# Top-2 choice by rank, with softmax weights and record addresses made on GpSimd, in a one-layer hybrid decoder kernel

## The reference, cut to what matters

```python
x = layer_norm(alpha * x + concat(attention, hgrn2) @ w_o, ln1_g, ln1_b)
g_prob = softmax(xt @ w_group + b_group)          # 4 groups
g_w, g_idx = top_k(g_prob, 1)
e_logits = expert logits of the chosen group      # 4 of 16 experts
e_w, e_idx = top_k(softmax(e_logits), 2)          # two experts
w_tok = g_w * e_w / sum(e_w)
for e in range(16):
    y += combine[:, e] * ((silu(xt @ w_gate[e]) * (xt @ w_up[e])) @ w_down[e])
x = layer_norm(alpha * x + y, ln2_g, ln2_b)
```

## Time and profile before

| | |
|---|---|
| median of 3 runs | 619.57 us (618.94 to 619.57) |
| the profiled execution | 618.28 us |
| its span, first to last instruction | 616.5 us |
| TensorE busy | 594.3 us (96%) |
| VectorE busy | 478.2 us (78%) |
| ScalarE busy | 373.8 us (61%) |
| GpSimd busy | 128.4 us (21%) |
| mean granted TensorE clock | 0.989 |

### The profile page before, as it was taken

How to read it: one execution, slowest core, us unless ns; L and a number is a source line. 1 busy time by engine, 2 the same in 40 slices (tenths; PEclk the granted TensorE clock), 3 DMA queues, 4 the chain that set the end, 5 groups by cost and what they waited for, 6 DMA issues and landing times.

```text
span 616.5 us, 9761 instructions
## 1 busy us (share of the span) xinstructions
PE 594.3 (96%) x3691; PEld 478.2 (78%) x3691; DVE 478.2 (78%) x572; ACT 373.8 (61%) x401; POOL 128.4 (21%) x111
## 2 busy tenths in 40 slices
PE   9999999999999999999799999999999999999990
PEld 7878888888887678877588888888888888888870
DVE  3758598794577765546898889888888988888867
ACT  3659434432215984213378887877887787787735
POOL 0004222290000440000483532111111011111000
PEclk9999999999999999999899999999999999999996
DMA  9831133223206003975699999999999999999664
GB/s 327 295 99 60 62 131 118 84 72 77 71 2 204 2 3 114 419 281 209 231 394 419 418 366 372 392 388 389 408 408 391 388 389 388 392 411 403 222 171 136
DMA packets 42557, 155.77 MB, mean 253 GB/s; under 512 B 11939, under 2 KB 12147, under 8 KB 30236
## 3 DMA queue, kind: packets, MB, share of 16 engines
q1 hardware_dynamic: 37500, 138.40, 57.4%
q0 software_dynamic: 5024, 16.92, 10.6%
HBM read 139.96 MB, written 15.34 MB: 252 GB/s over the span
## 4 chain that ended last, share of the span: by engine, by line
PE 87%; DMA 5%; DVE 4%; issue 2%; ACT 2%; DVEq 0%; POOLq 0%
PE psum L659 25%; PE psum L661 23%; PE psum L660 23%; DMA acc_dram<-misc,slots 3%; PE psum L772 2%; PE psum L1054 2%; PE psum L912 2%; PE psum L889 2%; DMA ring<-acc_dram 1%; PE psum L1071 1%; PE psum L876 1%; PE psum L668 1%; ACT ring L1313 1%; PE psum L814 1%; DMA misc<-x_dram,first 1%
## 5 line engine op out<-in xcount | busy, mean ns | idle before, releaser
L1776 DVE TENSOR_TENSOR w_lo<-ring,w_hi 128x2048 fp32r<-128x2048 f32 x95 | 216.5, 2294 | 23.7 <-ACT w_hi L1346 23.6
L659 PE MATMUL psum<-w_hi,act_hi 128*128 128x512 f32 x544 | 219.1, 403 | 1.5 <-DVE act_lo L1935 1.0
L661 PE MATMUL psum<-w_hi,act_lo 128*128 128x512 f32 x544 | 212.6, 391 | 0.0
L660 PE MATMUL psum<-w_lo,act_hi 128*128 128x512 f32 x544 | 212.3, 390 | 0.0
L1346 ACT ACTIVATE w_hi<-ring 128x2048 fp32r<-128x2048 f32 x96 | 182.1, 1916 | 25.1 <-PE psum L661 25.1
L659 PEld LDWEIGHTS psum<-w_hi,act_hi 128*128 128x128 f32 x544 | 102.3, 188 | 28.2 <-DVE w_lo L1776 4.7
L661 PEld LDWEIGHTS psum<-w_hi,act_lo 128*128 128x128 f32 x544 | 102.1, 188 | 22.1
L660 PEld LDWEIGHTS psum<-w_lo,act_hi 128*128 128x128 f32 x544 | 102.3, 188 | 19.2
L613 POOL DMA_INDIRECT acc_dram<-misc,slots x15 | 25.6, 1706 | 193.6 <-ACT misc L1396 176.0
L1194 ACT ACTIVATE w_hi<-ring 128x2048 fp32r<-128x2048 f32 x17 | 32.6, 1918 | 49.1 <-PE psum L661 47.4
L1505 DVE TENSOR_TENSOR w_lo<-ring,w_hi 128x2048 fp32r<-128x2048 f32 x17 | 39.8, 2344 | 22.3 <-ACT w_hi L1194 22.1
(11 more groups left out here) (246 smaller groups left out, 687.1 us busy)
## 6 DMA issues: line engine op xcount, KB each, us to landing
ring<-in_w_gate SPq DMA_DIRECT2D x32, 1024.0 KB, 17.4
ring<-in_w_up SPq DMA_DIRECT2D x32, 1024.0 KB, 18.3
ring<-in_w_down SPq DMA_DIRECT2D x32, 1024.0 KB, 18.7
ring<-in_w_in SPq DMA_DIRECT2D x13, 1024.0 KB
ring<-in_w_o SPq DMA_DIRECT2D x4, 1024.0 KB
acc_dram<-ring SPq DMA_DIRECT2D x5, 512.0 KB, 4.0
ring<-in_x SPq DMA_DIRECT2D x2, 1024.0 KB, 6.5
ring<-strip_dram SPq DMA_DIRECT2D x8, 256.0 KB, 4.4
```

The source lines that it names most:

```text
L659: pe.matmul(dst, lh, rh, start=first, stop=False, skip_group_check=True)
L660: pe.matmul(dst, lh, rl, start=False, stop=False, skip_group_check=True)
L661: return pe.matmul(dst, ll, rh, start=False, stop=last, skip_group_check=True)
L1776: dve.tensor_tensor(w_lo[:, v0 % WBUF, :], ring[:, slot, :], w_hi[:, v0 % WBUF, :].bitcast(F32), ALU.subtract).then_inc(s_lo, 1)
```

## The change

The choice is made by counting: for each value, how many of its group of four beat it (ties go to the earlier). Rank below 0.5 is the first choice, 1 the second, below 1.5 both. VectorE does this in three instructions per pair of tiles; the pair 0 and 1 goes ahead of the last half residual. GpSimd makes the exponents' input, the addresses and the weights' sum in a chain of 26 instructions behind gather 1, each of which waits for the one before it; ScalarE's Exp waits for the twelfth, VectorE's reciprocal (now ahead of unit 3) for the twenty-fifth. VectorE splits units 0 and 1 where it made weights and addresses. The diff, but for the offsets of the constants:

```diff
@@ -84,8 +84,8 @@
     for l, m in enumerate(LEVELS):
         c[:, C_MASK + 64 * (l + 1):C_MASK + 64 * (l + 2)] = (s // (2 * m) == t // (2 * m)) & (s % (2 * m) < m) & (t % (2 * m) >= m)
     c[:, C_SCAN:C_SCAN + SEQ] = (np.arange(SEQ) % CH != 0)[None]
-    c[:, C_W4:C_W4 + 4] = [4, 3, 2, 1]
-    c[:, C_E16:C_E16 + NE] = np.arange(NE)
+    c[:, C_TIE:C_TIE + 16] = [0 if i < j else np.finfo(np.float32).tiny for j in range(4) for i in range(4)]
+    c[:, C_E16:C_E16 + NE] = np.arange(NE) - NE
     for i in range(T):
         tok = i * P + np.arange(P)
         for k in range(2):
...
@@ -294,9 +294,13 @@
             return v.rearrange("p (%s) -> p %s" % (" ".join(names), " ".join(names)), **dict(zip(names, shape)))
 
         r_msk = msk_b[:, :].rearrange("p (i e) -> p i e", i=T)
-        r_l, r_hot, r_top, r_first = rcol(T, NL), rcol(T, NL), rcol(T * (1 + NG), 1), rcol(T * (1 + NG), 1)
-        r_l2, r_hot2, r_top2, r_first2 = rcol(T, NE), rcol(T, NE), rcol(T * NG, 1), rcol(T * NG, 1)
-        r_x, r_d, r_both, r_gsum, r_gw, r_q = rcol(T, NG + 1), rcol(T, NG), rcol(T, NE), rcol(T, 1), rcol(T, 1), rcol(T, 1)
+        r_l, r_group, r_hot, r_hot2, r_top = rcol(T, NL), rcol(T, NG), rcol(T, NE), rcol(T, NE), rcol(T, 1)
+        r_rank, r_beats, r_step = rcol(T, NL), rcol(2 * (1 + NG), 4, 4), rcol(T, NE)
+        r_x, r_gsum, r_q = rcol(T, NG + 1), rcol(T, 1), rcol(T, 1)
+        def four(v):
+            return v.rearrange("p t (g e) -> p t g e", g=NG)
+
+        group_four = r_group.rearrange("p t (g a) -> p t g a", a=1).broadcast_to((P, T, NG, EPG))
         r_sel, r_pos, r_t16, r_at1, r_adr, r_cnt = rcol(2, T, NE), rcol(T, NE), rcol(2 * T, NE), rcol(T, NE), rcol(2 * T, 1), rcol(1)
 
 
...
@@ -593,8 +597,49 @@
             pool.wait_ge(s_slots, 2)
             gather(1)
 
+            pooled = [2]
+
+            def then(ins):
+
+                pooled[0] += 1
+                ins.then_inc(s_pool, 1)
+                pool.wait_ge(s_pool, pooled[0])
+
+            def folded(v, n, op):
+
+                while n > 1:
+                    n //= 2
+                    then(pool.tensor_tensor(v(0, n), v(0, n), v(n, 2 * n), op))
+
+            pool.wait_ge(s_rneed, 1)
+            pooled[0] = 4
+            pool.wait_ge(s_pool, 4)
+            then(pool.tensor_tensor(r_x[:, :, 0:NG], r_l[:, :, 0:NG], r_top.broadcast_to((P, T, NG)), ALU.subtract))
+            then(pool.tensor_scalar(r_hot, r_rank[:, :, NG:NL], 0.5, None, ALU.is_lt))
+            then(pool.tensor_scalar(r_hot2, r_rank[:, :, NG:NL], 1.0, None, ALU.is_equal))
+            then(pool.tensor_tensor(four(r_sel[:, 0]), four(r_hot), group_four, ALU.mult))
+            then(pool.tensor_tensor(four(r_sel[:, 1]), four(r_hot2), group_four, ALU.mult))
+            then(pool.tensor_tensor(r_step, r_sel[:, 1], r_sel[:, 0], ALU.subtract))
+            then(pool.tensor_tensor(r_step, r_step, r_l[:, :, NG:NL], ALU.mult))
+            folded(lambda a, b: r_step[:, :, a:b], NE, ALU.add)
+            pool.tensor_copy(r_x[:, :, NG:NG + 1], r_step[:, :, 0:1]).then_inc(s_rneed, 1)
+
+            e16 = cst[:, C_E16:C_E16 + NE].rearrange("p (a e) -> p a e", a=1)
+            then(pool.tensor_scalar(r_pos, r_at1, float(NE), None, ALU.mult))
+            then(pool.tensor_tensor(r_pos, r_pos, e16.broadcast_to((P, T, NE)), ALU.add))
+            for k in range(2):
+                then(pool.tensor_tensor(r_sel[:, k], r_sel[:, k], r_pos, ALU.mult))
+            sel = r_sel.rearrange("p k i e -> p (k i) e")
+            folded(lambda a, b: sel[:, :, a:b], NE, ALU.add)
+            then(pool.tensor_copy(addr_i[:, :, :].rearrange("p k i -> p (k i)").rearrange("p (n a) -> p n a", a=1), sel[:, :, 0:1]))
+            pool.wait_ge(s_rexp, 1)
+            folded(lambda a, b: r_x[:, :, a:b], NG, ALU.add)
+            then(pool.tensor_scalar(r_q, r_x[:, :, NG:NG + 1], ALPHA, ALPHA, ALU.mult, ALU.add))
+            pool.tensor_tensor(r_gsum, r_x[:, :, 0:1], r_q, ALU.mult).then_inc(s_addr, 1)
+
             pool.wait_ge(s_pads, 16 * (SEQ // P))
             pool.wait_ge(s_addr, 2)
+            then(pool.tensor_tensor(weight_of(rec_i[:, :, 1, 2:3]), weight_of(rec_i[:, :, 0, 2:3]), r_x[:, :, NG:NG + 1], ALU.mult))
             for n in range(2 * T):
                 if n == 5:
                     pool.wait_ge(s_slots, 3)
...
@@ -1372,7 +1417,7 @@
             logit_copy(T - 1)
             for v0 in range(3):
                 ehi(v0, 0)
-            act.wait_ge(s_rneed, 1)
+            act.wait_ge(s_rneed, 2)
             act.activation(r_x, r_x, ACT.Exp).then_inc(s_rexp, 1)
 
             def xt_hi(e, b):
...
@@ -1817,6 +1862,18 @@
                     residual(T - 1, 0)
                 if i >= 1:
                     link(logits_of(i - 1))
+
+            def ranks(t0):
+
+                ls = r_l[:, t0:t0 + 2, :].rearrange("p t (g e) -> p (t g) e", e=4)
+                shape = (P, 2 * (1 + NG), 4, 4)
+                link(dve.tensor_tensor(r_beats, ls.rearrange("p s (a i) -> p s a i", a=1).broadcast_to(shape),
+                                       ls.rearrange("p s (j a) -> p s j a", a=1).broadcast_to(shape), ALU.subtract))
+                tie = cst[:, C_TIE:C_TIE + 16].rearrange("p (a j i) -> p a j i", a=1, j=4)
+                link(dve.tensor_tensor(r_beats, r_beats, tie.broadcast_to(shape), ALU.is_ge))
+                link(dve.tensor_reduce(r_rank[:, t0:t0 + 2, :].rearrange("p t (g e a) -> p (t g) e a", e=4, a=1), r_beats, AX.X, ALU.add))
+
+            ranks(0)
             residual(T - 1, 1)
             moments(T - 1)
             last_in, last_out = x_res[:, T - 1, :], x1_out[:, T - 1, :]
...
@@ -1829,40 +1886,20 @@
 
 
             tokens = cst[:, C_REC:C_REC + 6 * T].rearrange("p (i a b) -> p i a b", i=T, a=1)[:, :, :, 0:1]
-            def bc(ap, n):
-                return ap.broadcast_to((P, T, n))
-
             link(logits_of(T - 1))
-            w4 = cst[:, C_W4:C_W4 + 4].rearrange("p (a n) -> p a n", a=1)
-
-            def first_max(values, hot, top, first, n):
-
-                values, hot = values.rearrange("p t (g e) -> p (t g) e", e=4), hot.rearrange("p t (g e) -> p (t g) e", e=4)
-                link(dve.tensor_reduce(top, values, AX.X, ALU.max))
-                link(dve.tensor_tensor(hot, values, top.broadcast_to((P, n, 4)), ALU.is_equal))
-                link(dve.tensor_tensor(hot, hot, w4.broadcast_to((P, n, 4)), ALU.mult))
-                link(dve.tensor_reduce(first, hot, AX.X, ALU.max))
-                link(dve.tensor_tensor(hot, hot, first.broadcast_to((P, n, 4)), ALU.is_equal))
-
-            first_max(r_l, r_hot, r_top, r_first, T * (1 + NG))
-            link(dve.scalar_tensor_tensor(out=r_l2, in0=r_hot[:, :, NG:NL], scalar=-BIG, in1=r_l[:, :, NG:NL], op0=ALU.mult, op1=ALU.add))
-            first_max(r_l2, r_hot2, r_top2, r_first2, T * NG)
-            group = r_hot[:, :, 0:NG]
-
-            def in_group(dst, src):
-                four = lambda v: v.rearrange("p t (g e) -> p t g e", g=NG)
-                return dve.tensor_tensor(four(dst), four(src), group.rearrange("p t (g a) -> p t g a", a=1).broadcast_to((P, T, NG, EPG)), ALU.mult)
-
-            link(dve.tensor_tensor(r_both, r_hot[:, :, NG:NL], r_hot2, ALU.add))
-            in_group(r_msk, r_both).then_inc(s_mask, 1)
+            ranks(T // 2)
+            link(dve.tensor_scalar(r_group, r_rank[:, :, 0:NG], 0.5, None, ALU.is_lt))
+
+            dve.scalar_tensor_tensor(out=four(r_msk), in0=four(r_rank[:, :, NG:NL]), scalar=1.5, in1=group_four,
+                                     op0=ALU.is_lt, op1=ALU.mult).then_inc(s_mask, 1)
             dve.wait_ge(s_used, MIX_UNITS)
             dve.tensor_copy(record[:, :, :, :], tokens.broadcast_to((P, T, NE, 2))).then_inc(s_rec, 1)
             dve.wait_ge(s_mask, 1)
+            dve.tensor_reduce(r_top, r_l[:, :, 0:NG], AX.X, ALU.max)
             dve.wait_ge(s_pos, 1)
             pos = psum[:, 7, 0:T * NE].rearrange("p (i e) -> p i e", i=T)
-            e16 = cst[:, C_E16:C_E16 + NE].rearrange("p (a e) -> p a e", a=1)
-
-            link(dve.scalar_tensor_tensor(out=r_at1, in0=pos, scalar=1.0, in1=r_msk, op0=ALU.add, op1=ALU.mult))
+            dve.scalar_tensor_tensor(out=r_at1, in0=pos, scalar=1.0, in1=r_msk, op0=ALU.add, op1=ALU.mult).then_inc(s_rneed, 1)
+            dve.wait_ge(s_rneed, 1)
 
             def place(e):
 
...
@@ -1879,25 +1916,8 @@
             place(1)
             slots_of(0, 1, 5)
             slots_of(1, 2, 3)
-            tops = r_top.rearrange("p (t g) a -> p t (g a)", t=T)
-            link(dve.tensor_tensor(r_x[:, :, 0:NG], r_l[:, :, 0:NG], tops[:, :, 0:1].broadcast_to((P, T, NG)), ALU.subtract))
-            link(dve.tensor_tensor(r_d, r_top2.rearrange("p (t g) a -> p t (g a)", t=T), tops[:, :, 1:1 + NG], ALU.subtract))
-            link(dve.tensor_tensor(r_d, r_d, group, ALU.mult))
-            dve.tensor_reduce(r_x[:, :, NG:NG + 1], r_d, AX.X, ALU.add).then_inc(s_rneed, 1)
-            in_group(r_sel[:, 0], r_hot[:, :, NG:NL])
```

(20 more changed lines are left out.)

## The result

| | before | after |
|---|---|---|
| median, runs side by side | 619.57 us | 622.84 us (622.50 to 625.04) |
| ratio | | 1.0063, 95% interval 1.0045 to 1.0082 |
| profiled execution, span | 616.5 us | 621.0 us |

Slower by 3.3 us, where +6.7 was forecast.

The account below looks back on a forecast made before the run. TensorE, busy 96% of 616.5 us, bounds it through its hole before the experts. Gather 2's wait (336.5 - 329.84 = +6.7) swallows the first shift and clock: 619.57 + 6.7 = 626.3 us, range 620.9 to 631.0.

Parts of the forecast that it names:

- the first wait: Before the experts: ScalarE's Exp waits for twelve GpSimd instructions, holding e_hi to 306.8 against 303.60; experts start 3.2 us later.
- the hold-up by the splits: GpSimd can't reach its data during VectorE's big subtractions; its first small instruction sits behind unit 1's until 301.6.
- rival 1: Only the Exp wait counts, gather 2 lands in time: +3.2, with the clock +5.1, 621 to 625 us; chance 0.25.
- second wait: At expert 2's transposes: gather 2, behind five scatters, issued near 327.5, lands 336.5 against 329.84, +6.7 us.
- Choice by rank: Router mask on VectorE: 3.39 us removed, 1.5 put in, 1.9 less; 1.57 passes the warming matmuls.
- Start of GpSimd's chain: Behind gather 1, ending near 300.2 in unit 0's split; the first small instruction sits behind unit 1's until 301.6.
- rival 3: Gather 0 is itself caught by unit 0's split, lands 2.3 us late, first shift +4.1; counted into forecast and rival 1.
- Size of the twelve instructions: GpSimd's twelve ahead of Exp: six at 0.53, six at 0.25 + 0.09, 5.2 us; bounds 3.2 and 7.1.
- first shift: Start of the expert matmuls: 3.2 us later than before, 3.2 to 5.1 with the low clock.
- Clock: TensorE's pause grows by 4.8 us; a low stretch on expert matmuls, 3.8 us at half rate, loses 1.9 us.
- After that: Slots' table, queued behind gather 2, moves 7 to 11 us, its need 6.7; within 5.8 us, no further wait.
- Faster rival: GpSimd not held by splits, twelve done by 303.3: 0.85 us faster, up to 1.57; 618.0 to 618.7 us; chance 0.10.

Follow-up runs that it names:

- unit 1 late: The changed kernel with the split of unit 1 moved back behind the first e_lo: 627.42 us, ratio 1.0134.
- warm gap: The changed kernel with 40 more warming matmuls between the first transposes and the wait for the first e_lo: 628.31 us, ratio 1.0158.
- Exp behind e_hi: The changed kernel with Exp and its wait moved behind both e_hi copies on ScalarE: 630.58 us, ratio 1.0185.
- gather 2 ahead: Gather 2 behind two scatters instead of five: 626.29 us in the changed kernel, 621.31 in that with the warm gap, 624.86 in that with Exp behind e_hi.
- choice by rank with more warming: The changed kernel without GpSimd's chain (VectorE makes its values, unit 1 split after first e_lo), plus 14 warming matmuls: 617.27 us, second set 616.91.

## Why the prediction was right, and where its sizes were off

The direction, the first wait and the hold-up by the splits were right. That the time lies in the range is owed to the range's lower part, which was there for rival 1: the forecast's own case, a second wait that takes TensorE to +6.7, did not occur in the change, and gather 2 came in time by 0.7 us only because the low clock had slowed everything around it. To that extent it was luck.

- **Choice by rank.** The mask was forecast at 293.9, it ended at 293.91. Of the 1.9 us, 1.57 were to pass the warming matmuls; gather 0 was issued at 296.69 (296.92 forecast), so it was 1.8.
- **Start of GpSimd's chain.** Forecast: gather 1 to 300.2, first instruction until 301.6. Measured: 300.01 and 301.44. The caught-gather case of rival 3 didn't happen; gather 0 took 1.06 us.
- **Size of the twelve instructions.** The term was too large. The eleven free ones were priced at 4.9 us and took 3.8: 0.30 to 0.32 for a two-input instruction of 64 elements instead of 0.44, with 0.08 between two. The 443 ns of the earlier trace rows belong to a form with a pointer to a scalar; the nearest here, with a constant, took 0.38. So e_hi came at 305.53, not 306.8, and the first shift was 1.9 us, not 3.2. A two-input GpSimd instruction at 0.30 stands against VectorE's 0.22, 1.4 times. The Trainium skill, GPSIMD Engine Reference, section Engine selection, has about twice. For all twelve, with no split beside them, the kernel with unit 1 late shows 4.2 us (300.33 to 304.49), where my sum had 5.2 and the estimate from the Trainium skill's ratio 5.8.
- **Clock.** A low stretch on expert matmuls was priced at 1.9 us, measured 2.3. With the first shift of 1.9 that is the 4.1 to 4.2 us by which the transposes of expert 2 were late; rival 1 had such a case at 5.1, with a first shift of 3.2.
- **The step that failed is the size of the second wait.** "Gather 2 is issued near 327.5" was 4.5 us too late: scatters started at 313.49 instead of 315.5, and up to the next issue the five took 9.5 us instead of 12.0. Two things made the start early: the cheaper chain, and that in the change ScalarE, held back with TensorE at the low clock, gave the hi of unit 3 late, so that GpSimd's last product (312.73, 0.21 us) passed before that split (rows below). With unit 1 late the same product stood behind the split for 2.12 us and the scatters began at 316.19; with the warm gap at 315.40. Later two of the five scatters went through in 0.96, as the splits were spread. Landing took 10.3 us, not 9. It landed 0.7 us ahead of need, so the wait itself was nil. The mechanism is real in nearby kernels: it decided three experiments (warm gap, Exp behind e_hi, unit 1 late) with 4.7 to 8.0 us, and there gather 2 was issued at 326.37, 329.91 and 326.80, around the forecast's 327.5. For the change itself rival 1 was the case that came true; I gave it 0.25. The timeline of VectorE of the changed kernel, then of GpSimd with unit 1 late:
```profile
314.31 2.29 DVE L1821 TENSOR_TENSOR w_lo<-ring,w_hi 128x2048 fp32r<-128x2048 f32 x1 [1.73 <-ACT w_hi L1391]
```
```profile
313.78 2.12 POOL L642 TENSOR_TENSOR rec_i<-rec_i,misc 128x4 f32<-128x4 f32 x1 [0.36 <-DVE rec_i L1962]
316.19 1.08 POOL L591 DMA_INDIRECT slot_dram<-rec_i,addr_i  x1 [0.29 <-POOL rec_i L642]
```
- **After that.** That the table of slots is no further wait was right for the change, with 3.4 us of room; the 2.46 us with gather 2 ahead show how near it is.
- **Faster rival.** It needed the twelve done by 303.3; they were done at 305.37. Even without the hold-up by the splits (unit 1 late) they ended at 304.49.

## What to carry to other kernels

Moving small work to an idle engine changes what stands in that engine's queue and in the queues of those that wait for it: here Exp was not urgent, but the copy behind it was, and a gather stood behind the scatters that needed the results. Before moving a step, list for each queue what is next behind the wait, and when it is needed. When several waits lie close in line, removing the first alone can cost time, because it also takes away the gaps in which the later ones caught up. Edits had to go together here: Exp or the clock with gather 2 to win back what each alone had lost (both stayed above before), choice by rank with more warming to beat before.

## What the runs showed of the hardware

- GpSimd's small instructions stand still while VectorE subtracts two on-chip tensors: 1.40 us against 0.23 for the same instruction. With two splits back to back (unit 1 late, 306.47 to 311.0) one instruction came through per split: two sums of pairs, started at 306.63 and 308.94, took 2.23 and 2.15 us.
- The hold-up can also fall on VectorE: beside a GpSimd product of 1024 elements (2.88 us, from 351.90 in the change) a split took 3.79 us instead of 2.29:
```profile
351.39 3.79 DVE L1821 TENSOR_TENSOR w_lo<-ring,w_hi 128x2048 fp32r<-128x2048 f32 x1 [0.43 <-ACT w_hi L1391]
```
- A dependent GpSimd instruction costs 0.08 us between end and next start, and 0.19 (four elements) to 0.38 us (64 elements) itself.
- The granted clock of a stretch can fall in the warming matmuls too: 32 of them took 3.65 us in some executions and 5.2 to 5.3 in others of the same kernels, and the execution's time moves by 1 to 2 us with it (the change: 622.84 and 624.90; choice by rank with more warming: 617.01 and 618.79, in two sets of runs). That this is most of the spread of these kernels is likely but not shown, since few of the executions have a trace.
